# One expert layer in a two-block transformer kernel: tiles of 64 places in the two column halves of the array, weights used as plain float32, and seven overflow tiles placed between the others

## The reference

```python
N_EXPERTS, TOP_K_INNER, D_MODEL, D_EXPERT, SEQ = 32, 2, 1024, 512, 256

def hier_moe(h, w_router_group, b_router_group, w_router_expert, b_router_expert, w_gate, w_up, w_down):
    grp_logits = (h @ w_router_group) + b_router_group          # 4 groups of 8 experts
    grp = jnp.argmax(grp_logits, axis=-1)
    exp_logits = ((h @ w_router_expert) + b_router_expert).reshape(N, 4, 8)[tok_idx, grp]
    top_v, top_i = lax.top_k(exp_logits, 2)
    gate = grp_p * jax.nn.softmax(top_v, axis=-1)
    eid = (grp[:, None] * 8 + top_i).reshape(-1)                # 512 pairs of a token and an expert
    order = jnp.argsort(eid)
    ...
    def expert_block(args):
        xblk, e = args
        return (jax.nn.silu(xblk @ w_gate[e]) * (xblk @ w_up[e])) @ w_down[e]
    ...
    return y            # for each token the sum of its two experts' results, times their gates
```

## Time and profile before

| | us |
|---|---|
| median of 3 runs (3603.89 to 3606.3) | 3605.28 |
| the profiled execution: time | 3605.12 |
| the profiled execution: span of its core | 3603.3 |
| TensorE busy (matmuls) | 3177.5 |
| VectorE busy | 2555.8 |
| ScalarE busy | 1477.3 |
| GpSimd busy | 808.8 |
| mean granted TensorE clock | 0.915 |

### The profile page before, as it was taken

How to read it: one execution, slowest core, us unless ns; L and a number is a source line. 1 busy time by engine, 2 the same in 40 slices (tenths; PEclk the granted TensorE clock), 3 DMA queues, 4 the chain that set the end, 5 groups by cost and what they waited for, 6 DMA issues and landing times. The chain is left out here.

```text
span 3603.3 us, 50144 instructions
## 1 busy us (share of the span) xinstructions
PE 3177.5 (88%) x18738; PEld 2794.1 (78%) x18738; DVE 2555.8 (71%) x3325; ACT 1477.3 (41%) x1734; POOL 808.8 (22%) x356
## 2 busy tenths in 40 slices
PE   7948885869999996679989999997769989999997
PEld 7848774558888876568868999996649878999996
DVE  4564335289999984538967888886546977888887
ACT  3421113157777772322334444443333234444443
POOL 0011110034444430000002444441000001444442
PEclk9959775889999998689999999998879999999998
DMA  5400002069999926034135555554414315555553
GB/s 176 158 1 1 1 1 82 11 254 386 380 380 378 379 102 214 18 106 147 53 123 176 186 187 187 187 186 135 147 51 151 103 65 181 189 186 186 187 188 134
DMA packets 187380, 573.26 MB, mean 159 GB/s; under 512 B 23520, under 2 KB 89440, under 8 KB 162272
## 3 DMA queue, kind: packets, MB, share of 16 engines
q1 hardware_dynamic: 181616, 567.03, 44.4%
q0 software_dynamic: 5616, 4.21, 0.4%
HBM read 586.90 MB, written 19.40 MB: 168 GB/s over the span
## 5 line engine op out<-in xcount | busy, mean ns | idle before, releaser
L2206 POOL TENSOR_TENSOR u_low<-u_raw,u_top 128x1024 fp32r<-128x1024 f32 x192 | 463.8, 2416 | 1736.7 <-ACT u_top L2116 1736.7
L2034 PE MATMUL psum<-v_top,hid 128*128 128x512 f32 x1888 | 623.9, 393 | 18.1 <-DVE hid L2304 18.0
L2034 PE MATMUL psum<-h_parts,u_top 128*128 128x256 f32 x3072 | 561.0, 283 | 4.6 <-DVE h_parts L2344 4.6
L1439 DVE TENSOR_TENSOR piece_lows<-piece_raw,piece_tops 128x2048 fp32r<-128x2048 f32 x210 | 509.4, 2454 | 7.3 <-ACT piece_tops L1396 6.8
L2034 PEld LDWEIGHTS psum<-h_parts,u_top 128*128 128x128 f32 x3072 | 492.0, 192 | 20.3 <-DVE h_parts L2344 5.4
L2313 DVE TENSOR_TENSOR hid<-gelu,hid 128x256 fp32r<-128x256 f32 x192 | 473.8, 2467 | 6.6
L1396 ACT ACTIVATE piece_tops<-piece_raw 128x2048 fp32r<-128x2048 f32 x210 | 402.3, 1919 | 105.2 <-PE psum L1329 103.9
L2034 PE MATMUL psum<-h_parts,u_low 128*128 128x256 f32 x1536 | 435.2, 283 | 0.0
L2034 PEld LDWEIGHTS psum<-v_top,hid 128*128 128x128 f32 x1888 | 357.9, 190 | 91.1 <-issue 20.0
L2034 PE MATMUL psum<-v_low,hid 128*128 128x512 f32 x944 | 371.7, 394 | 0.0
L1329 PE MATMUL psum<-piece_tops,tile_cols 128*128 128x512 f32 x1120 | 361.6, 394 | 7.4 <-DVE piece_lows L1439 7.4
(11 more groups left out here) (497 smaller groups left out, 5717.8 us busy)
## 6 DMA issues: line engine op xcount, KB each, us to landing
v_raw<-expert_v_dram SPq DMA_DIRECT2D x236, 512.0 KB, 3.4
u_raw<-expert_u_dram SPq DMA_DIRECT2D x192, 512.0 KB, 4.4
piece_raw<-w_gate_dram SPq DMA_DIRECT2D x70, 1024.0 KB
piece_raw<-w_up_dram SPq DMA_DIRECT2D x70, 1024.0 KB
piece_raw<-w_down_dram SPq DMA_DIRECT2D x70, 1024.0 KB
in_raw<-w_in_dram SPq DMA_DIRECT2D x48, 1024.0 KB
all_gates<-expert_u_dram SPq DMA_DIRECT2D x64, 512.0 KB, 3.4
all_gates<-w_query_dram SPq DMA_DIRECT2D x16, 1024.0 KB
```

The costliest lines, as they stand in the source:

```text
L1439: nc.vector.tensor_tensor(r32(low[:, n % RING, :]), raw[:, n % RAW, :], top[:, n % RING, :], ALU.subtract).then_inc(piece_low, 1)
L2034: last = nc.tensor.matmul(out, r32(lhs[i]), r32(rhs[j]), start=start and n == 0, stop=stop and n == 2, skip_group_check=True)
L2206: nc.gpsimd.tensor_tensor(r32(low_u[:, k, :]), raw_u[:, k, :], top_u[:, k, :], ALU.subtract).then_inc(u_low_done, 1)
```

## The change

- A tile has 64 places instead of 128. An expert with more than 64 places gets up to three further tiles; over all experts there can be at most seven such tiles, and `route` finds them from a table of 3 x 32 entries (expert and depth) instead of 32.
- The stationary operand is 64 columns wide. The same tokens are loaded into both column halves of the array: half 0 multiplies them with the first half of a weight's columns and writes to partitions 0 to 63, half 1 with the second half of the columns and writes to 64 to 127. So the matmuls of gate and up have 256 moving columns and those of down 512, and they alternate between the halves.
- Weights, tokens and hidden values are plain float32; the high and low parts and their copies are gone. `sorted_cols` is added up over its parts in PSUM, 8 copies instead of 16.
- A piece's buffer is released by TensorE (`piece_used`), and there are 14 of them instead of 6. The first 14 pieces are loaded during `route`.
- The seven overflow tiles stand between the others, one after each fourth expert from the sixth on (`TILE_ORDER`).
- SyncE reads 14 values in place of 6. The results of a tile are copied by VectorE alone, into two banks in turn, and go to HBM as half rows. The gathers at the end have a buffer of their own.

```diff
-OVERFLOW = CHOSEN * T // (P + 1)
+OVERFLOW = CHOSEN * T // (P // 2 + 1)
...
                 for c in range(KD):
+                    if c >= 4:
+                        pe.wait_ge(sorted_dve if c % 2 else sorted_act, c // 2 - 1)
                     for part in range(2):
-                        n = 2 * c + part
-                        if n >= 4:
-                            pe.wait_ge(sorted_dve if part else sorted_act, n // 2 - 1)
                         for a in range(NT):
-                            last = nc.tensor.matmul(PS[:, 4 + n % 4, :], r32(parts[:, part, a, c * P:(c + 1) * P]),
-                                                    r32(slot_hot[:, a, :]), start=(a == 0), stop=(a == NT - 1))
-                        last.then_inc(sorted_done, 1)
+                            last = nc.tensor.matmul(PS[:, 4 + c % 4, :], r32(parts[:, part, a, c * P:(c + 1) * P]),
+                                                    r32(slot_hot[:, a, :]), start=(part == 0 and a == 0),
+                                                    stop=(part == 1 and a == NT - 1))
+                    last.then_inc(sorted_done, 1)
...
+                for m in range(DEEPER):
+                    past = float((m + 1) * SLOTS_OF_TILE)
+                    nc.vector.tensor_scalar(deep[:, 0, m, :], start[:, 0:EXPERTS], past, None, ALU.add)
+                    nc.vector.tensor_scalar(deep[:, 1, m, :], count[:, 0:EXPERTS], past, None, ALU.subtract)
+                    last = nc.vector.tensor_copy(deep[:, 2, m, :], C["iota"][:, 0:EXPERTS])
+                step(last)
...
-                for table, past in ((start, float(P)), (count, float(-P))):
+                for i, to in enumerate((start[:, EXPERTS:], count[:, EXPERTS:], over_id[:, 1, :])):
                     step(nc.vector.tensor_tensor(over_part[:, :, :], over_hot[:, :, :],
...
-RAW, RING = 6, 4
+RAW = 14
+SLOTS_OF_TILE = P // 2
 TILES = EXPERTS + OVERFLOW
+
+
+def tiles_in_order():
+
+    order = []
+    for e in range(EXPERTS):
+        order.append(e)
+        if e % 4 == 1 and e > 4:
+            order.append(EXPERTS + (e - 5) // 4)
+    return order
...
                 for n in range(RAW, PIECES):
-                    sp.wait_ge(piece_low, n - RAW + 1)
-                    tile = piece_of(n)[0]
+                    sp.wait_ge(piece_used, n - RAW + 1)
+                    tile = TILE_ORDER[piece_of(n)[0]]
...
                 def into_hidden(t, q, bank):
                     n = place_of(t, q)
-                    pe.wait_ge(piece_low, n + 1)
+                    pe.wait_ge(S["piece_in"][n % RAW], 16 * (n // RAW + 1))
                     for c in range(4):
-                        k, s = q % 2 * 4 + c, slice(c * BANK, (c + 1) * BANK)
-                        last = three_passes(PS[:, bank, :], (window[:, t % 2, 0, k, :], window[:, t % 2, 1, k, :]),
-                                            (top[:, n % RING, s], low[:, n % RING, s]), k == 0, k == KD - 1)
+                        k = q % 2 * 4 + c
+                        for g in range(2):
+                            at = c * DE + g * WIDE
+                            last = nc.tensor.matmul(PS[side(g), bank, 0:WIDE], window[:, t % 2, k, :],
+                                                    raw[:, n % RAW, at:at + WIDE], start=(k == 0), stop=(k == KD - 1))
                     last.then_inc(piece_used, 1)
...
-                    for f in range(FC):
-                        last = nc.tensor.transpose(PS[:, TURNED, f * P:(f + 1) * P], hid[:, f * P:(f + 1) * P], C["ident"])
+                    for j in range(2):
+                        last = nc.tensor.transpose(PS[:, TURNED, j * P:(j + 1) * P], hid[:, j * P:(j + 1) * P], C["ident"])
...
                         for c in range(2):
-                            f = (q - 4) * 2 + c
-                            for h in range(2):
-                                s = slice(c * D + h * BANK, c * D + (h + 1) * BANK)
-                                last = three_passes(PS[:, OUT[h], :], (hid_cols[:, 0, f, :], hid_cols[:, 1, f, :]),
-                                                    (top[:, n % RING, s], low[:, n % RING, s]), f == 0, f == FC - 1)
+                            for g in range(2):
+                                at = c * D + g * HALF
+                                last = nc.tensor.matmul(PS[side(g), OUT[t % 2], :], hid_cols[:, c, q - 4, :],
+                                                        raw[:, n % RAW, at:at + HALF], start=(q == 4 and c == 0),
+                                                        stop=(q == 5 and c == 1))
...
-                    for part in range(2):
-                        last = nc.gpsimd.tensor_copy(r32(window[:, t % 2, part, :, :]), r32(G[:, part, :, bass.ds(at, P)]))
-                    last.then_inc(window_done, 1)
+                    nc.gpsimd.tensor_copy(window[:, t % 2, :, :], G[:, :, bass.ds(at, SL)]).then_inc(window_done, 1)
```

More of the change, by code:

```diff
@@ L1236, in _ @@
+                step(nc.vector.tensor_copy(S["over_expert"][:, 0:OVERFLOW], over_id[:, 1, :]))
                 step(nc.vector.tensor_copy(S["tile_start"][:, :], start[:, :]))
-                step(nc.vector.tensor_scalar(absent[:, :], count[:, :], C["row"], float(1 << 20), ALU.is_le, ALU.mult))
-                step(nc.vector.scalar_tensor_tensor(absent[:, :], start[:, :], C["row"], absent[:, :], ALU.add, ALU.add))
+                step(nc.vector.tensor_scalar(absent[:, :], count[:, :], C["row"][:, 0:1], float(1 << 20), ALU.is_le, ALU.mult))
@@ L1240, in _ @@
+                step(nc.vector.scalar_tensor_tensor(absent[:, :], start[:, :], C["row"][:, 0:1], absent[:, :], ALU.add, ALU.add))
+                step(nc.vector.tensor_scalar(absent[:, :], absent[:, :], 2.0, C["row"][:, 1:2], ALU.mult, ALU.add))
                 nc.vector.tensor_copy(S["tile_rows"][:, :], absent[:, :])
-                for c in range(KD):
-                    dve.wait_ge(sorted_done, 2 * c + 2)
-                    nc.vector.tensor_copy(r32(G[:, 1, c, 0:ROWS]), PS[:, 5 + 2 * (c % 2), :]).then_inc(sorted_dve, 1)
@@ L1250, in piece_of @@
+TILE_ORDER = tiles_in_order()
 def piece_of(n):
@@ L1271, in load_piece @@
     tile, q = piece_of(n)
-    e = tile if expert is None else expert
+    e = TILE_ORDER[tile] if expert is None else expert
     src = S["dram"][("w_gate", "w_gate", "w_up", "w_up", "w_down", "w_down")[q]]
@@ L1482, in _ @@
                         rows = S["x"][:, a, :]
-                        last = nc.vector.scalar_tensor_tensor(rows, raw[:, a, k * D:(k + 1) * D], S["share"][:, a, k:k + 1], rows,
+                        last = nc.vector.scalar_tensor_tensor(rows, back[:, a, k, :], S["share"][:, a, k:k + 1], rows,
                                                               ALU.mult, ALU.add)
@@ L1517, in _ @@
                         nc.gpsimd.indirect_dma_start(
-                            out=raw[:, a, k * D:(k + 1) * D], out_offset=None, in_=result[:, :],
+                            out=back[:, a, k, :], out_offset=None, in_=result[:, :],
                             in_offset=bass.IndirectOffsetOnAxis(ap=S["place"][:, a, k:k + 1], axis=0),
```

178 lines of the change are left out of this document (67 added, 111 removed).

## The result

| | us |
|---|---|
| before, beside the runs of the changed kernel: median (lowest to highest) | 3604.59 (3603.48 to 3606.3) |
| after: median of 4 runs (lowest to highest) | 3477.65 (3473.69 to 3482.16) |
| ratio, 95% interval | 0.9648 (0.9631 to 0.9665) |
| the profiled execution after: time / span | 3476.19 / 3474.4 |

The forecast was 3469 us. Between the profiled executions 128.9 us went. The second block's first matmul, 1380.57 in the earlier trace rows, now starts at 1250.23, 130.3 us earlier; the part behind it took 1.4 us longer. That part isn't touched, and in the profiled executions of all these kernels it takes from 2219.9 to 2227.2 us.

A forecast was written before the change was run, and what follows sets the result against it. TensorE, not the busy DMA engines, was taken to bound the kernel. After: TensorE 1221 us, DMA 1211, plus 3 us, last matmul 1224; second block at 1245 instead of 1380.6; 3605.1 - 136 = 3469 us, range 3448 to 3515 (82%).

The forecast's parts named there:

- a piece, with a full queue: Weight loads of the experts' stage: 1.049 MB at the burst's 426 GB/s, 2.47 us a piece, 14.8 us an expert.
- TensorE's tile: Experts' matmuls: 10.5 us of streams and transposes plus what stands beside them, 11.7 us a tile, 39 tiles 456 us.
- from there to the next block: Tail after the last matmul (result copy, scatter, gathers, additions, barriers): left as before, 20.9 us.
- The bound now: Experts' stage before the change: TensorE sets the pace at 16.7 us a tile; DMA engines at 380 GB/s aren't at their limit.
- beside its streams: Tile time outside the matmul streams: 0.9 us from the kernel before, plus 0.3 us for changes between halves and full width.
- now the one and now the other: End of the stage: TensorE (1221 us) and DMA (1211 us) are close and wait in turn, 3 us added.
- The transfers' end: Weight loads: 178 pieces x 2.47 = 440 us from about 767 us, ending at 1207 us.
- The halves: Experts' matmuls: two with 64 stationary columns each, in different partition halves, run at once at full speed; 10.5 us a tile.
- (b): Rival: halves don't run at once when the half changes with every matmul; tile 22 us, 3868 us; 7%.
- The start: Routing: +2 us (bounds -1 and +6), window copy -3 us, 14 register reads 8.3 us; first matmul about 760.6 us.
- (a): Rival: DMA engines were at their limit after all, 2.76 us a piece, stage ends at 1284 us, 3508 us; 12%.
- (d): Rival: loads stop while the seven overflow tiles without an expert run; 82 us on top of the DMA's time, 3538 us; 5%.

The follow-up runs named there:

- half the bytes: Changed kernel with each load bringing only the first half of its piece (0.5 MB), all matmuls reading that half, so wrong weights: 3433.83 us, ratio 0.9527.
- one half alone: Changed kernel with all expert matmuls writing to partitions 0 to 63, as many and as long, half of the results missing: 3839.02 us, ratio 1.0653.
- late reads: Changed kernel with SyncE reading an overflow tile's two register values just before that tile's loads, instead of all 14 at the start: 3475.2 us, ratio 0.9642.
- grouped order: Changed kernel loading 0.5 MB of each piece (wrong weights), with each piece's matmuls of half 0 first, then those of half 1: 3484.61 us, ratio 0.9666.
- the kernel without absent tiles: Changed kernel with the seven overflow tiles, which have no expert in these inputs, not computed; tables and register reads stay: 3469.18 us, ratio 0.9627.

## Why the prediction was right, and where not

| step | predicted | measured |
|---|---|---|
| first matmul | 760.6 | 760.06 |
| 15th piece issued | 767 | 766.41 |
| a piece, with a full queue | 2.47 us | 2.50 us (419 to 420 GB/s) |
| last weight in | 1207 | 1225.5 |
| TensorE's tile, when it never waits | 11.7 us | 10.95 us (half the bytes) |
| last matmul ends | 1224 | 1229.5 |
| from there to the next block | 20.9 us | 20.7 us |
| next block | 1245 | 1250.2 |

**The bound now.** Right in the reading of the earlier trace rows: the busy DMA engines were not at their limit. The kernel with six buffers shows it, and the changed one moves 419 GB/s for 450 us. The Trainium skill (DMA: Bandwidth & Descriptors, Where 436 GB/s comes from) bounds loads from HBM at about 358 GB/s per core; by that the kernel would have come out near 3538 us, and the trace disagrees with its 419 to 420. The same page of the Trainium skill (Bandwidth, Measured) gives about 358 GB/s as the share of a core when both cores of an HBM domain stream; here only one core ran.

**TensorE's tile.** The streams were sized rightly at 10.5 us. The step that failed is the 1.2 us "beside its streams", carried over from the kernel before: in the middle of the stage 10.8 less 10.5 leaves 0.3 us. The whole stage with half the bytes takes 427.2 us, its slower start included, so TensorE would have ended at 760.6 + 427.2 = 1188 us instead of 1221. The prediction had put it ahead of the transfers as the later of two close ends, and that order was wrong: the transfers bind alone, and the 3 us for "now the one and now the other" name a mechanism that hardly acts.

**The transfers' end.** Mis-sized by 18.5 us, from four terms. The sustained pace is 420 and not the burst's 426 GB/s: 178 pieces take 444.4 instead of 440 us; the first packet starts 1.0 us after its issue; the result writes share the engines, 2.1 MB, 5.0 us; and 8.6 us are left. 766.4 + 1.0 + 444.4 + 5.0 + 8.6 = 1225.4. Of these 8.6 us some 6 are the thinning out: the three rows from 1210 to 1225 us fall short of 420 GB/s by 2.6 MB. The prediction had looked at the writes only as a wait for their buffer, not as bytes, and had ended the last piece as if it were one in the middle. The two errors have opposite signs, TensorE 33 us too late and the transfers 18.5 too early, and so the next block's start was missed by 5.2 us only; the time stands by luck closer than its terms. The forecast's other 3.5 us to the median of 3477.65 are the part behind (1.4 us longer), the roundings, and the 1.5 us by which the profiled execution lies under the median.

**The halves.** Right, and decisive: one half alone gives 3839 us where rival (b) had worked out 3868. The rule of the Trainium skill (TensorE: Matmul & The Clock Gate, part 3), by which a weight load overlaps with running matmuls only when the row group differs, would have made each weight load cost time, since all matmuls here use all rows. The starts in the earlier trace rows as well as the 0.216 us between pairs show no such cost in strict alternation, and neither do the same steps of 0.216 us in one half alone. The grouped order, in which most neighbours share a half, is the one that loses.

**The start.** The routing's new selection took 0.86 us an operation against 0.26, as worked out, and the last sorted copy began 2 us later, at 757.0 instead of 754.9. The 14 reads took 0.57 us each instead of 0.59, and they do stand before all issues; with the late reads the loads ended 2.8 us earlier, of which the earlier first matmul accounts for 1.3.

**The rivals.** (a) 2.76 us a piece: fell with 2.50. (b) fell with one half alone. (c) the clock: 1.00 from 800 to 900 us, 0.98 from 1100 to 1200 with TensorE busy 90 of 100 us; nothing of the 50 us. (d) absent tiles not hidden: fell when leaving them out won 3.6 to 8.5 us instead of 82.

## What to carry to other kernels

A share of busy DMA engines near 1 doesn't show that they are at their limit (here 0.98 stood beside 400 GB/s, and 1.01 beside 419): compare the GB/s with those of a burst that has no buffers to wait for, and deepen the ring before you believe in a bound. When only 64 stationary columns have work in them, two halves of the array on different moving columns double the pace of plain float32 (10.9 us a tile against 21.2), if the order alternates strictly; in groups it was 12.1 us, and the format alone would have lost. Once the transfers bind, count every byte on them, and place the work that loads nothing between the work that does, neither so early that the transfers fall short (as two executions here suggest) nor so late that it stands behind the last load.

## What the runs showed of the hardware that was not expected

- Two column halves of plain float32 keep their full pace each (entries of 256 columns in pairs every 0.216 us), but in groups of eight entries of one half a tile takes 12.1 instead of 10.8 us.
- At the end of a long series of loads the 16 DMA engines don't end together: the last megabyte takes 8.15 us, 6.2 without the result writes, 5.5 with the written rows moved to other partitions in every second tile, against 2.8 in the middle. With six buffers in place of fourteen it takes 3.4.
- The transfers hold 426 GB/s in a burst of 14 pieces and 419 to 420 over 450 us.
- In the kernel without absent tiles TensorE waited for weights in gaps of at most 2.2 us and was busy 84.24 us from 800 to 900 us, at a granted clock of 1.00, its upper level of 2.4 GHz. From 1000 to 1100 us it was busy 78.71 us, at a granted clock of 0.98.
